# Seven half-size products on TensorE: four and four operand sums in place of five and five, and products added up in three PSUM banks

## The reference, cut to what matters

```
x = x + gate * (y @ w_out)                 # w_out1, w_sgu_out0, w_rwkv_out, w_mla_out, w_sgu_out3
u, g = split(h @ w_up); g2 = silu(conv3(u)) * conv3(g)          # feed-forward, 22 column tiles each
u, z = gelu(h @ w_u), silu(h @ w_z); s = u * mixed * z          # SGU mixer of layer 3, 16 tiles each
r, k, v, z = xs[c] @ w_in[c]  for c in 0..3                     # RWKV features, 8 tiles for each c
```

## Time and profile before

| | |
|---|---|
| median of 3 runs | 5179.44 us (5175.92 to 5180.61) |
| profiled execution, first to last instruction | 5180.3 us |
| TensorE busy | 4703.1 us (91%) |
| VectorE busy | 2631.4 us (51%) |
| ScalarE busy | 1240.5 us (24%) |
| mean granted clock of TensorE | 0.958 |

### The profile page before, as it was taken

The page is one execution under the profiler, slowest core; times in us unless marked ns, Lnnn a source line. Parts: engine busy times, 40 slices in busy tenths (PEclk is TensorE's granted clock), DMA queues, the critical chain, the costliest instruction groups (busy, mean ns, idle before and its releaser), DMA issues.

```text
span 5180.3 us, 72699 instructions
## 1 busy us (share of the span) xinstructions
PE 4703.1 (91%) x29226; PEld 3006.8 (58%) x29226; DVE 2631.4 (51%) x4682; ACT 1240.5 (24%) x2309; POOL 660.3 (13%) x894
## 2 busy tenths in 40 slices
PE   7987798899999999999979856899898999999998
PEld 3556645444688444555545445888654555455687
DVE  2447755655688021334376486455624444333465
ACT  2223413410111021111010264222112434201230
POOL 0014400000000000110000042655100000000000
PEclk9999999999999999999999967999999999999999
DMA  4322151134222111222112257344211101021222
GB/s 151 102 86 82 62 179 39 41 134 171 73 89 86 67 53 57 92 101 91 37 63 100 106 202 227 91 115 110 62 53 42 36 28 37 25 90 67 79 78 82
DMA packets 152503, 451.26 MB, mean 87 GB/s; under 512 B 73200, under 2 KB 73456, under 8 KB 130800
## 3 DMA queue, kind: packets, MB, share of 16 engines
q1 hardware_dynamic: 128464, 350.91, 20.2%
q0 software_dynamic: 22848, 92.29, 5.2%
q10 hardware_dynamic: 864, 3.47, 0.2%
HBM read 377.42 MB, written 69.21 MB: 86 GB/s over the span
## 4 chain that ended last, share of the span: by engine, by line
PE 66%; issue 10%; DVE 8%; POOLq 5%; PEld 4%; DVEq 2%; ACT 2%; DMA 2%; POOL 1%; PEldq 0%; SPq 0%; ACTq 0%
PE psum L389 49%; PE psum L2043 5%; PEld psum L389 4%; POOLq L3071 2%; POOLq L3069 2%; PE psum L714 2%; PE psum L2430 1%; DVE sbuf L1229 1%; PE psum L2622 1%; PE psum L2621 1%; PE psum L2593 1%; DVE sbuf L2768 1%; PE psum L1167 1%; PE psum L761 1%; PE psum L1391 1%
## 5 line engine op out<-in xcount | busy, mean ns | idle before, releaser
L389 PE MATMUL psum<-sbuf 128*128 128x256 f32 (+3 forms) x9328 | 2937.9, 473 | 100.2 <-DVE sbuf L1764 32.6
L389 PEld LDWEIGHTS psum<-sbuf 128*128 128x128 f32 (+1 forms) x9328 | 1754.3, 190 | 1236.0 <-issue 905.3
L3681 PE MATMUL psum<-sbuf 64*64 64x64 f32 (+1 forms) x10752 | 427.4, 238 | 28.7 <-SPq L3590 18.0
L3681 PEld LDWEIGHTS psum<-sbuf 64*64 64x64 f32 x10752 | 412.6, 138 | 46.1 <-SPq L3590 20.2
L2043 PE MATMUL psum<-sbuf 128*128 128x512 f32 x640 | 280.1, 600 | 18.1 <-issue 18.1
L631 DVE CUSTOM_DVE_ANT_0 sbuf<-sbuf 128x1024 f32<-128x1024 f32 x160 | 196.2, 1226 | 137.4 <-DMA sbuf<-w_side 101.8
L1776 DVE SCALAR_TENSOR_TENSOR sbuf<-psum,sbuf 128x256 f32<-128x256 f32 (+2 forms) x288 | 125.9, 480 | 209.7 <-PE psum L389 204.4
L2043 PEld LDWEIGHTS psum<-sbuf 128*128 128x128 f32 x640 | 122.7, 192 | 175.6 <-issue 174.5
L3806 ACT ACTIVATE sbuf<-psum 128x256 f32<-128x256 f32 (+3 forms) x384 | 128.5, 367 | 362.4 <-PE psum L3681 299.0
L697 ACT ACTIVATE sbuf<-sbuf 128x512 f32<-128x512 f32 (+1 forms) x104 | 54.4, 558 | 539.6 <-DVE sbuf L1776 355.8
L3070 POOL TENSOR_TENSOR sbuf<-sbuf 96x30 f32<-96x30 f32 (+14 forms) x240 | 138.7, 578 | 52.1 <-issue 18.8
(11 more groups left out here) (332 smaller groups left out, 5256.2 us busy)
## 6 DMA issues: line engine op xcount, KB each, us to landing
sbuf<-w_side POOLq DMA_DIRECT2D x128, 512.0 KB, 3.9
sbuf<-w_sgu_uz SPq DMA_DIRECT2D x32, 1088.0 KB, 5.0
sbuf<-terms SPq DMA_DIRECT2D x115, 256.0 KB, 2.9
sbuf<-w_up SPq DMA_DIRECT2D x22, 1024.0 KB, 4.9
sbuf<-w_merge SPq DMA_DIRECT2D x8, 2560.0 KB, 9.0
sbuf<-w_mla_head SPq DMA_DIRECT2D x16, 1152.0 KB, 5.1
sbuf<-w_sgu_v SPq DMA_DIRECT2D x8, 2048.0 KB, 7.9
sbuf<-w_sgu_out SPq DMA_DIRECT2D x8, 2048.0 KB, 8.2
```

The lines of the kernel that those rows point to most:

```text
L389: last = nc.tensor.matmul(out, w, x, start=(n == 0), stop=(n == len(pairs) - 1))
L3681: last = t.matmul(out[hs], lhs[hs], rhs[hs], start=start, stop=stop)
```

## The change

The seven products are formed in the other way, with four sums of weight quarters and four of token quarters, where the second and the fourth sum build on an earlier one. The products run in the order 1, 2, 6, 5, 7, 3, 4 and add up in PSUM: product 6 is added to product 1 in the same bank after that has been read, and product 7 to both; product 3 is added to product 5; product 4 to 1, 6 and 7. Three banks hold a step, and steps alternate between two sets of three. Each product is read once: in the residuals by one VectorE add, elsewhere products 1, 6, 5 and 4 by a ScalarE copy and 2, 7 and 3 by a VectorE add. A product that goes on in a bank waits for the read of what the bank held (`first` or `added`); between it and the product before in that bank stands one other product.

```diff
+class Seven:
+    ORDER = (1, 2, 6, 5, 7, 3, 4)
+    A_PLAIN = {1: (0, 0), 2: (0, 1), 4: (1, 1)}
+    B_PLAIN = {1: (0, 0), 2: (1, 0), 3: (1, 1)}
+    SUMS = (5, 6, 7, 3)
+    TERMS = (5, 6, 7, 4)
+    BANK = {1: 0, 6: 0, 7: 0, 4: 0, 2: 1, 5: 2, 3: 2}
+    OPENS = (1, 2, 5)
+    RESULT = {1: (0, 0), 2: (0, 0), 6: (0, 1), 3: (0, 1), 5: (1, 1), 7: (1, 1), 4: (1, 0)}
+    COPIED = (1, 6, 5, 4)
+    ADDED = (2, 7, 3)
+    def bank(p, n):
+        return 3 * (p % 2) + Seven.BANK[n]
+    def a_operands(n, a, s):
+        return {5: (a(1, 0), a(1, 1), ALU.add), 6: (s.get(5), a(0, 0), ALU.subtract), 7: (a(0, 0), a(1, 0), ALU.subtract),
+                3: (a(0, 1), s.get(6), ALU.subtract)}[n]
...
+def seven_products(nc, out, pairs, n):
+    for i, (w, x) in enumerate(pairs):
+        last = nc.tensor.matmul(out, w, x, start=(i == 0 and n in Seven.OPENS), stop=(i == len(pairs) - 1), skip_group_check=True)
...
 # residual, tensor
-                if p > 0:
-                    pe.wait_ge(self.added, 7 * (p - 1) + i + 1)
+                if n == 1 and p >= 2:
+                    pe.wait_ge(self.added, 7 * (p - 1))
+                if n == 6:
+                    pe.wait_ge(self.added, 7 * p + 1)
+                if n in (7, 3, 4):
+                    pe.wait_ge(self.added, 7 * p + i - 1)
...
-            pe.drain().then_inc(self.w.used(p % 2), 1)
 # residual, vector: before the steps, and then in them
+        a_sum(0, 5)
+        b_sum(5)
+        dve.drain()
+        a_sum(0, 6)
+        b_sum(6)
+        add(0, 0, 1)
+        b_sum(7)
+        a_sum(0, 7)
+        dve.drain()
+        a_sum(0, 3)
+        b_sum(4)
         for p in range(KD // 2):
...
+                if (p, i) != (0, 0):
+                    dve.drain()
+                    add(p, i, n)
+                if more and n == 5:
+                    a_sum(p + 1, 5)
+                if more and n == 7:
+                    a_sum(p + 1, 6)
+                if more and n == 3:
+                    a_sum(p + 1, 7)
+                if more and n == 4:
+                    a_sum(p + 1, 3)
+            dve.sem_inc(self.w.used(p % 2), 1)
 # feed-forward, tensor; the SGU and the RWKV features have the same waits
+                if n == 1 and j >= 2:
+                    pe.wait_ge(self.first, 4 * (j - 1))
+                if n == 2 and j >= 2:
+                    pe.wait_ge(self.added, 3 * (j - 1))
+                if n in (6, 7, 3):
+                    pe.wait_ge(self.first, 4 * j + (6, 7, 3).index(n) + 1)
+                if n == 4:
+                    pe.wait_ge(self.added, 3 * j + 2)
...
-            pe.drain().then_inc(self.w.used(j % 2), 1)
 # feed-forward, scalar
+            for i, n in enumerate(Seven.ORDER):
+                if n in Seven.COPIED:
+                    act.wait_ge(self.products_done, 7 * j + i + 1)
+                    a.activation(self.quarter(j, *Seven.RESULT[n]), self.chip.bank(Seven.bank(j, n), self.WIDTH), ACT.Copy).then_inc(self.first, 1)
+                if n == 5 and j >= 1:
+                    silu(j - 1)
+            act.sem_inc(self.w.used(j % 2), 1)
 # feed-forward, in Norm.vector
         if i == self.HALF - 1:
-            self.a_sum(dve, 0, 2)
+            self.a_sum(dve, 0, 5)
+        if i == KD - 2:
+            self.b_sum(dve, 5)
         if i == KD - 1:
-            self.a_sum(dve, 0, 5)
+            dve.drain()
+            self.a_sum(dve, 0, 6)
 # feed-forward, vector
         for j in range(KF):
...
+            add(j, 1, 2)
+            if j >= 1:
+                dve.wait_ge(self.first, 4 * j)
+                convolve(j - 1, 1)
+            if more:
+                dve.wait_ge(self.products_done, 7 * j + 4)
+                self.a_sum(dve, j + 1, 5)
+            dve.drain()
+            add(j, 4, 7)
+            if more:
+                self.a_sum(dve, j + 1, 6)
+                self.a_sum(dve, j + 1, 7)
+            if j >= 1:
+                gate(j - 1)
+            add(j, 5, 3)
+            dve.drain()
+            if more:
+                self.a_sum(dve, j + 1, 3)
+            convolve(j, 0)
 # SGU, gpsimd
-            if j >= 2:
-                pool.wait_ge(self.mixed, j - 1)
-            self.nc.gpsimd.tensor_tensor(self.staged_v[j % 2], self.v[:, j], over(self.inv, P), ALU.mult).then_inc(self.staged, 1)
+            self.nc.gpsimd.tensor_tensor(self.v[:, j], self.v[:, j], over(self.inv, P), ALU.mult).then_inc(self.staged, 1)
```

More of the change, by code:

```diff
@@ L1770, in add @@
+            v.tensor_tensor(self.b_sums[n], first, second, op).then_inc(self.b_ready, 1)
         def add(p, i, n):
-            dve.drain()
             dve.wait_ge(self.summed, 7 * p + i + 1)
-            for half, j, sign in self.RESULTS[n]:
-                m = p + KD // 2 * half
-                for x, gates, cols in self.pieces[j]:
-                    last = v.scalar_tensor_tensor(x[:, m], self.chip.bank(i)[:, cols], gates[sign][:, m:m + 1], x[:, m], ALU.mult, ALU.add)
+            half, j = Seven.RESULT[n]
@@ L1876, in scalar @@
                 act.wait_ge(self.convolved, j - 1)
-            for i, n in enumerate((2, 5)):
-                act.wait_ge(self.products_done, 7 * j + i + 1)
-                for half, part, sign in S.RESULTS[n]:
-                    last = a.activation(self.quarter(j, half, part), self.chip.bank(i, self.WIDTH), ACT.Copy, scale=float(sign))
-                last.then_inc(self.first, 1)
-            if j >= 1:
-                silu(j - 1)
+            for i, n in enumerate(Seven.ORDER):
+                if n in Seven.COPIED:
[3 more added lines that the diff above has]
+                    silu(j - 1)
@@ L1915, in gate, with convolve @@
+        def convolve(j, n):
+            last = conv3(self.nc, dve, self.acc[j % 2][n], self.raw[j % 2][n],
+                         [self.chip.vec("ffn_w", 2 * KF * k + KF * n + j, 1) for k in range(3)], TL)
+            if n == 1:
+                last.then_inc(self.convolved, 1)
         def gate(j):
@@ L2300, in scalar @@
                 act.wait_ge(self.gated, j - 1)
[L2301 to L2307 removed]
+            for i, n in enumerate(Seven.ORDER):
+                if n in Seven.COPIED:
+                    act.wait_ge(self.products_done, 7 * j + i + 1)
+                    a.activation(self.quarter(j, *Seven.RESULT[n]), self.chip.bank(Seven.bank(j, n), self.width), ACT.Copy).then_inc(self.first, 1)
+                if n == 5 and j >= 1:
+                    activate(j - 1)
@@ L3962, in features @@
         spare = [A_W + u * WSLOT + 2 * KG * P for u in range(2)]
[L3963 removed]
+        norm = norm2(chip, layer, None, rows=both_rows(stages[0]), host=stages[0], by_host=6, banks=[7, 6],
                      few=dict(slots=spare, roots=[SGU_V + KG * T + 5 * KG // 2 * T // 2, spare[0] + T]))
```

557 lines of the change are left out of this document (282 added, 275 removed).

## The result

| | before | after |
|---|---|---|
| median, range (4 runs each) | 5179.4 us, 5175.92 to 5180.61 | 5145.91 us, 5142.88 to 5147.7 |
| ratio, 95% interval | | 0.9937 (0.9925 to 0.995) |
| profiled execution, span | 5180.3 us | 5145.9 us |

The kernel became 33.5 us faster, where 20 were forecast. A second timing of the same kernel gave 0.9933 (0.992 to 0.9947).

What follows compares the result with a forecast made beforehand. TensorE's own product time was taken as the bound. Drains at -18.0 us plus the starts and ends summed to -20.2, taking the profiled 5180.3 to 5160.1 us, 5159 on the median's scale (chance 0.73); range 5150 to 5173.

Steps and rivals of the forecast that it cites:

- The drains: Boundaries between steps in the changed stretches: removing drains closes all 66 gaps, -18.0 us; bounds 0 and -18.0.
- 12.36 us apart: Expected sign in the chain of waits: feed-forward steps run on without a break at this spacing, where it was 12.62.
- VectorE: Feed-forward steps: busy about 8.9 of 12.4 us, where it was 11.8; total down by about 22 x 3 us.
- New waits: Products continuing in a bank wait for its read: hidden under TensorE, cost 0, at least 0.8 of 1.77 us spare.
- Weights: Weight slots given back 0.7 to 1.7 us later, but first sum wanted only after product 5: cost 0.
- Starts of the residuals: First steps of five residuals: w_out1 +1.0 us, three with 8 tiles -1.4 each (-4.2), w_rwkv_out -0.8.
- the bound that the prediction had named: Four residual starts other than w_out1: each late by 1.2 us if the clock stays up, but 1.5 or more returns.
- Feed-forward: Start +1.1 us, a sum ahead of the norm's last row, nothing late after it; end -1.9, convolution instructions moved under product 4.
- SGU and features: SGU start +0.1 us (TensorE 0.9 earlier, sums late), SGU end +1.5 (gelu's table behind a copy), features' end +1.0.
- Rival 1: Bank handovers within steps: the reading engine is late for the next product, +38 us, about 5198 us; chance 0.08.
- Rival 2: Step boundaries: gaps stay because something other than the drain holds the first product, only -2 left, 5177 us; chance 0.08.
- Rival 3: Starts and ends worse: sums late in four other residuals (7.6 us), 1.2 GHz spells at two starts (3), 5170 us; chance 0.11.

Runs made afterwards that it cites:

- e4: Changed kernel with the feed-forward's first three products reordered to 1, 6, 2, so product 6 directly follows product 1 in its bank; 5168.99 us, ratio 0.9966.
- e2: Kernel before with its seven banks and sums kept, but no drain: VectorE gives weight slots back after product 7's last read; 5153.19 us, ratio 0.9936.
- e5: Changed kernel with starts and ends reordered (residual adds, feed-forward token sum, GpSimd's tiles, early gelu table load); 5136.81 us, ratio 0.9911.
- e8: The changed kernel unaltered, timed again on the same chip beside the later runs; 5147.01 us, ratio 0.9933.
- e1: Changed kernel with a bare TensorE drain put back at the end of each step of the five changed loops; 5168.22 us, ratio 0.9969.
- e3: Changed kernel with a drain after each of the seven products of a feed-forward step; 5222.42 us, ratio 1.0073.
- e6: Changed kernel with the drain in layer 0's SGU steps (16) dropped and its signal put on the last product; 5140.9 us, ratio 0.9923.
- e7: Changed kernel with the edits of e5 and e6 together; 5136.73 us, ratio 0.9908.

## Why the prediction was off, point by point

**The drains: -18.0 forecast, -33 measured.** This is the step that failed: the term "5.4 + 4.7 + 3.9 + 5 x 0.8 = 18.0 us in 66 boundaries" and its bound of the same size, "Bounds: 0 [...] and -18.0". That the drains were the cause was right, and so was the count. The price was taken from the waits alone, 0.26, on the argument that a feed-forward step is "one unbroken piece of TensorE work", 12.36 us. That piece is 56 records that start 0.216 apart, but it is shown to the *modelled* end of the last, and a record reads 0.378 to 0.379 long, in both kernels. The 0.16 by which a record's shown length exceeds the pitch counts at the end of each piece. And the second record after a drain comes 0.08 late inside the piece. 0.26 + 0.16 + 0.08 = 0.50, the saving of the table. The Trainium skill says that TensorE's end is an estimate of the profiler ("Perfetto Trace Analysis", Tensor Engine Instruction (MATMUL, LD_WEIGHTS)); the trace fits that, with records that read 0.379 long and start 0.216 apart.

The same misreading stands in the prediction a second time: it divided a piece by its records (12.36 / 56 = 0.2207) and took that for TensorE's pace. The pace is 12.11 / 56 = 0.2163, and so the steps did not run on "12.36 us apart", as it expected to see, but 12.11. And a third time in the first steps, where each wait for a sum was priced at its idle time: w_out1's first step shows 1.73 us of waits and is 2.3 longer than the others.

**VectorE.** Its busy time in a feed-forward step fell from 11.2 to 8.2 us (107.80 and 82.31 in 121 us, by steps of 12.62 and 12.11), the 3 us that were forecast. One reading on the way was wrong: the step of before has eight adds, not nine (176 in 22 steps; the 71 of the earlier trace rows come from a window that isn't a whole number of steps), so 11.8 was some 0.5 too much. Nothing hangs on it.

**New waits: 0 forecast, 0 measured.** No step but a first has one. The spare time of at least 0.8 us of 1.77 was right by what e4 shows for ScalarE: 0.87 of 1.73 is the handover, restart included, and 0.86 spare.

**Weights: 0.** Right: no wait for a load in the changed steps. e2 shows what cover this rests on.

**Starts of the residuals.** In w_out1 two waits of 0.62 and 1.11 against 0.7 and 1.2 forecast. For the three with 8 tiles I had said "so the sums are not late", because of a lower clock. In w_mla_out the clock did not fall, in after or in any later trace of the changed kernel: the windows view has PEclk 1.00 where the earlier trace rows has 0.52, and the timeline shows that the sum was late:

```profile
4591.00:4593.00 2.00, 2.00 (x11) 1.75 (x10) 1.94 (x1) 0.00 (x0) 0.00 (x0) 1.00 1.00 426
```

```profile
4589.47 7.17 PE L1706 MATMUL psum<-sbuf 128*128 128x256 f32 x32 [1.52 <-DVEq L4101]
...
4597.01 5.22 PE L1706 MATMUL psum<-sbuf 128*128 128x256 f32 x23 [0.37 <-DVE sbuf L1802]
```

0.37 here and 0.83 later, 1.2 in all, and the slow clock gone: the bound that the prediction had named ("if the shorter idle time keeps the clock up"). The first step is 1.8 us longer than the others in after, by its waits, and was 1.7 longer in before, by the clock, so the two cancel and the earlier start is what is left. TensorE had been idle 2.94 before this stage in before and 1.52 in after. That this is the reason is likely and not shown. Why two other residuals still start at PEclk 0.50, after 5.3 and 6.0 us of idle time, was not tried.

**Feed-forward.** End -1.9 forecast: TensorE's idle time before the next stage went from 7.00 to 5.08, -1.9. Start +1.1 forecast: the wait for the norm's last row went from 1.28 to 2.33, +1.05, but "After it nothing is late" missed what the longer wait set off. Windows of 2 us from the end of this wait on, in after and then in e5, where the same wait is 1.38 (the clock is the third number from the end):

```profile
1421.00:1423.00 2.00, 1.98 (x8) 1.67 (x9) 1.87 (x10) 0.39 (x1) 0.00 (x0) 0.82 0.00 0
1423.00:1425.00 2.00, 2.00 (x6) 1.65 (x5) 1.91 (x4) 0.00 (x0) 0.00 (x0) 0.50 0.00 0
1425.00:1427.00 2.00, 2.00 (x9) 1.66 (x9) 1.45 (x2) 0.39 (x1) 0.00 (x0) 0.83 0.00 0
```

```profile
1414.00:1416.00 2.00, 1.74 (x8) 1.43 (x8) 1.87 (x11) 0.59 (x2) 0.00 (x0) 1.00 0.00 0
1416.00:1418.00 2.00, 1.50 (x8) 1.14 (x7) 2.00 (x3) 0.00 (x0) 0.00 (x0) 1.00 0.00 0
1418.00:1420.00 2.00, 2.00 (x11) 1.75 (x10) 1.91 (x3) 0.38 (x1) 0.00 (x0) 1.00 0.00 0
```

After waits of 0.87 and 2.33 us with 8 records between them the granted clock falls to 0.50, that is 1.2 GHz, and six records stand in 2 us instead of eleven; the same stands in e8, e1 and e3 (and in e4, with a wait of 3.87). Products 2 and 6 of the first step, 1.73 us each at the full clock, took 2.4 and 2.9 us: +1.8 us that no term held. In before (wait 1.28) and in e5 (1.38) the clock stayed.

But the long wait doesn't settle it. e6 has the same instructions, the same 8 records and the same waits of 0.87 and 2.33 there, and kept its clock:

```profile
1420.00:1422.00 2.00, 1.57 (x7) 1.41 (x8) 1.88 (x11) 0.76 (x2) 0.00 (x0) 1.00 0.00 0
1422.00:1424.00 2.00, 2.00 (x10) 1.73 (x10) 2.00 (x3) 0.00 (x0) 0.00 (x0) 1.00 0.00 0
1424.00:1426.00 2.00, 2.00 (x11) 1.75 (x10) 1.83 (x4) 0.45 (x2) 0.00 (x0) 1.00 0.00 0
```

Its first step takes 14.79 us, where after, and e8, have 16.47. So the spell costs 1.7 us, and it came in four of the five executions with these two waits and not in the fifth. The start of w_out1 shows the same with one wait: 2.32 us in all traces of the changed kernel and of its variants, after which the clock fell in e1, e4, e6 and e7 and stayed in after, e3, e5 and e8. What decides between them was not found. The sum of 1.22 us put ahead of the last row thus cost 1.1 us for certain, its own wait, and 1.7 more where the clock fell; e5 got 1.9 of these 2.8 back against e8, and e7 only 0.2 against e6, since with the sum behind the row a wait of 0.50 comes later in the step.

**SGU and features.** TensorE started 1.0 earlier in the SGU (0.9 forecast). The start shows 0.27 (which the view puts down to "issue", and which e5's order did not change) and 1.09 of waits against 0.3 and 0.7 forecast, with the contention that had been read off: a sum of 1024 columns takes 1.22 us alone and 2.06 with GpSimd at work.

```profile
4825.88 1.22 DVE L2374 TENSOR_TENSOR sbuf<-sbuf 128x1024 f32<-128x1024 f32 x1
...
4827.27 18.59 POOL L2304 TENSOR_TENSOR sbuf<-sbuf 128x512 f32<-128x512 f32 x14 [406.69 <-DVE sbuf L2403]
4827.68 2.06 DVE L2374 TENSOR_TENSOR sbuf<-sbuf 128x1024 f32<-128x1024 f32 x1
...
4836.34 7.16 PE L1706 MATMUL psum<-sbuf 128*128 128x256 f32 x32 [1.09 <-DVE sbuf L2380]
```

The forecast had overlooked that before had a spell of the lower clock here too (PEclk 0.50), which after hasn't, at PEclk 1.00 from 4823 to 4831:

```profile
4850.00:4852.00 2.00, 2.00 (x6) 1.62 (x5) 2.00 (x2) 0.66 (x2) 2.00 (x2) 0.50 0.26 104
```

Its first step was 1.7 longer than the others in before by this spell, and is 1.9 longer in after by the waits; start and first step together came to -0.7 where +0.1 was forecast.

At its end gelu's table comes behind the copy, as forecast, and gelu starts 1.8 us after the last product where it was 0.5, +1.3 for a forecast of +1.5:

```profile
5033.45 0.39 ACT L2358 ACTIVATE sbuf<-psum 128x256 f32<-128x256 f32 x1 [0.93 <-PE psum L1706]
...
5033.91 1.28 ACT L2349 ACT_TABLE_LOAD   x1
5035.21 0.63 ACT L2349 ACTIVATE sbuf<-sbuf 128x512 f32<-128x512 f32 x1
```

At the features' end TensorE is idle 0.8 us longer than in before, for a forecast of +1.0.

All starts and ends together, by stretch. A stretch runs from the last untouched record of TensorE before it to the first after; what is left after taking off boundaries times the saving of the table above is the starts and ends:

| stretch | forecast: drains, rest | measured: whole | drains | rest |
|---|---|---|---|---|
| w_out1, feed-forward | -6.2, +0.2 | -10.3 | -12.2 | +1.9 |
| w_sgu_out0, features | -5.5, -0.4 | -10.3 | -9.1 | -1.2 |
| w_rwkv_out | -0.8, -0.8 | -2.2 | -1.5 | -0.7 |
| w_mla_out | -0.8, -1.4 | -3.3 | -1.5 | -1.8 |
| SGU layer 3, w_sgu_out3 | -4.7, +0.2 | -10.6 | -9.0 | -1.6 |
| sum | -18.0, -2.2 | -36.7 | -33.3 | -3.4 |

The rest was off by 1.2 us in sum and by 0.1 to 1.8 in its parts, the drains by 15.3. The +1.9 of the first row is the forecast +0.2 with the 1.7 of the clock. Of the -1.2 in the second row 0.8 are the three boundaries of the features that had cost more in before. The -1.6 of the last row holds the -0.7 of the SGU's start and -0.5 in the first step of w_sgu_out3. The untouched stages gave back 2.3 us in this pair of executions, so the spans differ by 34.4.

**The rivals.** Rival 1 (handovers cost) didn't come; e4 shows its price and that one product in between covers it. Rival 2 (the gaps stay) didn't either. Rival 3 came in part: the sums were late in w_mla_out too, and a spell of 1.2 GHz came at the feed-forward start, while one went at w_mla_out's and one at the SGU's. All are small beside the drains.

## What to carry to other kernels

Price a drain or any stop of TensorE by the starts of the records on both sides, or by the number of records in equal windows, never by the idle time alone: the busy column hides the modelled end of the last record. Put the signal on the last product instead of on a drain where an engine behind it reads the result anyway; each such drain in a TensorE-bound loop cost 0.42 to 0.50 us here. But count what the new releaser waits for: in e2 a release behind VectorE's last add closed a round of load, sum and adds that was longer than the step. Where the last wait before a loop grows, look at the granted clock behind it, in more than one execution. A PSUM bank can be read and then added to by the next product in it, provided that one other product, longer than the handover, lies in between.

## What was not expected of the hardware

- A drain between two products costs 0.42 us on average (e3, seven in a step: 0.37 or 0.45 by the place), 0.46 (e1, one at a step's end) to 0.50 us (with a signal on it, in the kernel before), of which 0.11 to 0.26 are idle time in the profile. The second record after it starts 0.29 us after the first instead of 0.216, in e1 and in most of e3's boundaries as in before. The last 0.04 between e1 and before lie in the idle time (0.22 and 0.26); where they come from was not settled. The drain that e6 removed, which had a signal on it, was worth 0.48.
- An uncovered handover of a bank from TensorE through ScalarE and back costs 0.87 us, though the copy takes 0.38.
- A wait of TensorE can cost more than itself: 2.33 us, shortly after one of 0.87, was followed by a granted clock of 0.50 and 1.7 us more in the next two products in after, e1, e3 and e8, and by neither in e6, with the same waits. Waits of 1.28 to 1.38 at the same place were followed by neither, in four traces (before, e2, e5, e7).
- Stages that nobody touched vary by up to 23 us in sum between executions of kernels that differ elsewhere (e1 and e3), more than the starts and ends together were worth. In this kernel small terms can be told only in the traces.
- A load that VectorE's own release starts, and that VectorE then waits for, can run later each step before TensorE shows a wait: in e2 the first came after ten steps.
